# A hybrid mLSTM/GLA decoder block: the first MLP product as seven block products for eight

## What is computed

```python
hm = rmsnorm(x, mlp_norm_g[l]) @ w1[l]          # 1024 -> 4096
x = x + jnp.square(jax.nn.relu(hm)) @ w2[l]     # 4096 -> 1024
return rmsnorm(x, final_norm_g)
```

## Time and profile before

| what | value |
|---|---|
| runs | 2822.79, 2825.96, 2828.97 us; median 2825.96 |
| profiled execution | span 2824.3 us; the runs shown lie 1.5 us under to 4.7 us over it |
| PE / PEld busy | 2800.3 (99%) / 2330.9 us (83%) |
| DVE / ACT / POOL busy | 1812.8 (64%) / 1514.2 (54%) / 1057.3 us (37%) |
| DMA | 393.41 MB, mean 139 GB/s |

### The profile page before, as it was taken

One profiled execution on the slowest core, in us unless ns is written; L12 is line 12 of the kernel. 1 busy time (PEld: TensorE's weight loads), 2 busy tenths in 40 slices (PEclk: granted clock), 3 DMA queues, 4 the chain that ended last, 5 costly groups with the idle time before them and its releaser, 6 DMA issues.

```text
span 2824.3 us, 44962 instructions
## 1 busy us (share of the span) xinstructions
PE 2800.3 (99%) x15076; PEld 2330.9 (83%) x15076; DVE 1812.8 (64%) x3011; ACT 1514.2 (54%) x3126; POOL 1057.3 (37%) x1334
## 2 busy tenths in 40 slices
PE   8999999999999999999999999999999999999998
PEld 8888888788878888888888888888888888888887
DVE  6376774766686755457687674466668675545665
ACT  6554444556555444556565554465655644455553
POOL 5264574644345500234546320044435550023440
PEclk9999999999999999999999999999999999999999
DMA  6732586555552222355654222255556222234442
GB/s 217 249 105 68 175 292 235 186 173 147 150 196 83 73 93 90 100 177 153 175 164 145 74 83 90 90 157 169 144 150 201 83 73 93 90 102 144 150 149 82
DMA packets 185906, 393.41 MB, mean 139 GB/s; under 512 B 14224, under 2 KB 14368, under 8 KB 185664
## 3 DMA queue, kind: packets, MB, share of 16 engines
q1 hardware_dynamic: 160112, 309.89, 35.8%
q0 software_dynamic: 22880, 75.72, 8.0%
q10 hardware_dynamic: 2672, 4.76, 0.4%
HBM read 346.24 MB, written 33.59 MB: 134 GB/s over the span
## 4 chain that ended last, share of the span: by engine, by line
PE 97%; DVE 1%; issue 1%; DMA 1%; ACT 0%; DVEq 0%; POOL 0%; ACTq 0%
PE bank L1975 44%; PE work L1975 22%; PE bank L2342 17%; PE work L2342 3%; PE work L1989 1%; PE bank L2380 1%; PE work L2091 1%; PE bank L1989 1%; PE work L2129 1%; PE work L2037 1%; PE work L2151 1%; PE work L2240 1%; PE work L2244 1%; PE work L2239 1%; PE work L2223 1%
## 5 line engine op out<-in xcount | busy, mean ns | idle before, releaser
L899 ACT ACTIVATE w_hi<-raw 128x512 fp32r<-128x512 f32 x1156 | 724.7, 630 | 1018.9 <-PE bank L1975 515.8
L1413 DVE TENSOR_TENSOR w_lo<-raw,w_hi 128x512 fp32r<-128x512 f32 x657 | 475.8, 728 | 792.9 <-ACT w_hi L899 791.4
L1411 DVE SCALAR_TENSOR_TENSOR w_lo<-raw,w_hi 128x512 fp32r<-128x512 f32 x499 | 448.1, 918 | 95.3 <-ACT w_hi L899 94.1
L734 POOL TENSOR_TENSOR hr<-qk 128x256 f32<-128x256 f32 x60 | 44.3, 738 | 790.0 <-ACT qk L1287 790.0
L2342 PE MATMUL bank<-w_hi,h_hi 128*128 128x512 f32 x720 | 280.3, 389 | 0.1
L2342 PE MATMUL bank<-w_lo,h_hi 128*128 128x512 f32 x720 | 280.1, 389 | 0.0
L2342 PE MATMUL bank<-w_hi,h_lo 128*128 128x512 f32 x720 | 280.1, 389 | 0.0
L1975 PE MATMUL bank<-w_hi,x_hi 128*128 128x512 f32 x640 | 255.2, 399 | 0.0
L1975 PE MATMUL bank<-w_lo,x_hi 128*128 128x512 f32 x640 | 249.6, 390 | 0.0
L1975 PE MATMUL bank<-w_hi,x_lo 128*128 128x512 f32 x640 | 249.4, 390 | 0.0
L724 POOL TENSOR_TENSOR h_lo<-qk,h_hi 128x256 fp32r<-128x256 f32 x180 | 188.0, 1064 | 67.2 <-ACT h_hi L1300 67.2
(11 more groups left out here) (399 smaller groups left out, 6473.6 us busy)
## 6 DMA issues: line engine op xcount, KB each, us to landing
raw<-in_w_dram SPq DMA_DIRECT2D x226, 512.0 KB, 3.9
raw<-sums_dram SPq DMA_DIRECT2D x120, 512.0 KB, 3.8
raw<-in_w_in_dram SPq DMA_DIRECT2D x112, 512.0 KB, 3.6
raw<-in_w_out_dram SPq DMA_DIRECT2D x32, 512.0 KB, 4.1
raw<-kq_dram SPq DMA_DIRECT2D x32, 512.0 KB, 3.7
raw<-vo_dram SPq DMA_DIRECT2D x32, 512.0 KB, 3.7
xres<-in_x_dram POOLq DMA_DIRECT2D x16, 512.0 KB, 6.1
early_rows<-in_w_dram POOLq DMA_DIRECT2D x8, 1024.0 KB, 9.1
```

Source lines behind the costliest of these rows:

```text
L734: nc.gpsimd.tensor_tensor(diff[:, kt, :], quarter(0, 0, kt), quarter(0, 1, kt), ALU.subtract).then_inc(diff_ready, 1)
L899: nc.scalar.activation(w_hi[:, slot, :], raw[:, pair_slot, slot % 2, :], ACT.Copy).then_inc(slab_hi, 1)
L1411: ins = stt(out=w_lo[:, slot, :], in0=src, scalar=1.0, in1=hi, op0=ALU.mult, op1=ALU.subtract)
L1413: ins = tt(w_lo[:, slot, :], src, hi, ALU.subtract)
```

## The change

w1 gets what w2 had. A pass now has 28 slabs of w1 (seven products by four slabs) and 28 of w2; a w1 slab is used with 12 matmuls of 256 columns (`w1_product`), since x is cut into token halves of 256. x is turned into `xg` (f32), and in pass 0 POOL and ACT make its combinations and their parts once per group (`x_first_sums`, `x_later_sums`, `x_high`, `x_low`), DVE two of the low parts. Chained products share PSUM banks. Hidden is put together from them: ACT copies P1, P7 and P6 (`copy_product`), DVE adds P2, P5 and P4 (`add_hidden`), ReLU and square are DVE's in pass 0 (`squared_relu`) and ACT's in the other passes (`relu_pair`, `square_pair`); P3 is ACT's ReLU and DVE's square. In `hidden_sums` POOL also makes the low parts of P1. DVE's low parts of P7 move behind the start of the w2 product.

POOL now has 32 jobs of sums: four at the end of the prologue (before the mixer's distances), two between distances and products of the mixer (their buffer is xres, reloaded after them), sixteen through `early_rows`, six after `hidden_sums(0)`, four after `hidden_sums(1)`. `next_rows` and all 16 moves of `next_blocks` come before the `hidden_sums` in which they stood. The last pass of group 3 has w1 in seven products and w2 plain.

```diff
+W2_AT = PRODUCTS * HALF
+PASS_SLABS = 2 * W2_AT
...
-EARLY_SUMS, BEFORE_SUMS = 8, 14
+N_SUMS = 2 * HB * HALF
+ROWS_SUMS, FIRST_SUMS, BEFORE_SUMS, NEXT_SUMS = 4, 6, 22, 28
 Q_P1, Q_P7, Q_P6, Q_P2, Q_P5, Q_P4, Q_P3 = range(PRODUCTS)
...
-DVE_LOW = {Q_P1: 0, Q_P7: 1, Q_P2: 2}
-POOL_LOW = {Q_P6: 0, Q_P5: 1, Q_P4: 2, Q_P3: 3}
+WEIGHTS = (("plain", 0, 0), ("sums", 1, 1), ("sums", 0, 0), ("plain", 1, 0), ("sums", 0, 1), ("sums", 1, 0),
+           ("plain", 1, 1))
+DVE_LOW = {Q_P7: 0, Q_P2: 1}
...
+                if n < FIRST_SUMS:
+                    return xres[:, 2 * (n % 2):2 * (n % 2) + 2, :]
+                if n < BEFORE_SUMS:
+                    return early_rows[:, n % 4]
+                if n < NEXT_SUMS and n % 4 >= 2:
+                    return tok[:, 2 * (n % 2):2 * (n % 2) + 2, :]
...
+            def sums_by_two(first, last):
+                for n in range(first, last):
+                    weight_sums(n)
+                    if n + 1 < last and n > first:
+                        sums_done(pool, n - 1)
+                        load_quarters(n + 1)
+            pool.wait_ge(tok_ready, PRO_ROWS)
+            for n in range(2):
+                load_quarters(n)
+            sums_by_two(0, ROWS_SUMS)
...
+                def x_first_sums():
+                    for kt in range(HALF):
+                        pool.wait_ge(xg_ready, KT * g + kt + 1)
+                        nc.gpsimd.tensor_tensor(xdiff[:, kt, :], xg_quarter(0, 0, kt), xg_quarter(1, 0, kt),
+                                                ALU.subtract).then_inc(x_s3_ready, 1)
+                    for kt in range(HALF):
+                        x_low(Q_P1, kt, xg_quarter(0, 0, kt))
+                    for kt in range(HALF):
+                        pool.wait_ge(x_s3_ready, HALF * g + kt + 1)
+                        x_low(Q_P7, kt, xdiff[:, kt, :])
+                def x_later_sums():
+                    pool.wait_ge(x_op_lo_pool, N_X_POOL * g + HALF)
+                    for kt in range(HALF):
+                        pool.wait_ge(xg_ready, KT * g + HALF + kt + 1)
+                        pool.wait_ge(x_s3_ready, HALF * g + kt + 1)
+                        nc.gpsimd.tensor_tensor(xg_quarter(1, 0, kt), xg_quarter(1, 0, kt), xg_quarter(1, 1, kt),
+                                                ALU.add).then_inc(x_s1_ready, 1)
+                        pool.wait_ge(x_s1_ready, HALF * g + kt + 1)
+                        nc.gpsimd.tensor_tensor(xg_quarter(0, 0, kt), xg_quarter(1, 0, kt), xg_quarter(0, 0, kt),
+                                                ALU.subtract).then_inc(x_s2_ready, 1)
+                    pool.wait_ge(x_op_lo_pool, N_X_POOL * g + 2 * HALF)
+                    for kt in range(HALF):
+                        pool.wait_ge(x_s2_ready, HALF * g + kt + 1)
+                        nc.gpsimd.tensor_tensor(xdiff[:, kt, :], xg_quarter(0, 1, kt), xg_quarter(0, 0, kt),
+                                                ALU.subtract).then_inc(x_s4_ready, 1)
+                    for kt in range(HALF):
+                        x_low(Q_P5, kt, xg_quarter(1, 0, kt))
+                    for kt in range(HALF):
+                        x_low(Q_P4, kt, xg_quarter(1, 1, kt))
+                    for kt in range(HALF):
+                        pool.wait_ge(x_s4_ready, HALF * g + kt + 1)
+                        x_low(Q_P3, kt, xdiff[:, kt, :])
...
+                def hidden_sums(hb):
                     if hb >= 1:
                         pool.wait_ge(operand_hi, per_pass(g, N_HIGH, hb, 0))
                         pool.wait_ge(operand_lo_pool, per_pass(g, N_POOL_LOW, hb, 0))
                     for kt in range(HALF):
-                        pool.wait_ge(hidden_ready, per_pass(g, KT, hb, kt + 1))
+                        operand_low(Q_P1, hb, kt, quarter(0, 0, kt))
+                    for kt in range(HALF):
+                        block_ready(pool, g, hb, Q_P2, kt // 2)
+                        block_ready(pool, g, hb, Q_P4, kt // 2)
                         nc.gpsimd.tensor_tensor(diff[:, kt, :], quarter(0, 0, kt), quarter(0, 1, kt),
                                                 ALU.subtract).then_inc(diff_ready, 1)
-                    if between is not None:
-                        between()
-                    pool.wait_ge(operand_lo_dve, per_pass(g, N_DVE_LOW, hb, HALF))
+                    pool.wait_ge(operand_lo_pool, per_pass(g, N_POOL_LOW, hb, HALF))
...
+                if first:
+                    for n in range(ROWS_SUMS, FIRST_SUMS):
+                        sums_done(pool, n - 2)
+                        load_quarters(n)
+                    sums_by_two(ROWS_SUMS, FIRST_SUMS)
+                    for n in range(ROWS_SUMS, FIRST_SUMS):
+                        sums_done(pool, n)
+                    for i in range(NCH):
+                        pool.dma_start(xres[:, i, :], A["x"][i * P:(i + 1) * P, :]).then_inc(x_in, 16)
...
-                    for n in range(4):
+                    for n in range(FIRST_SUMS, FIRST_SUMS + 4):
                         load_quarters(n)
-                    for n in range(EARLY_SUMS):
+                    for n in range(FIRST_SUMS, BEFORE_SUMS):
+                        if n == FIRST_SUMS + 10:
+                            pool.wait_ge(pr_ready, 8 * g + 8)
                         weight_sums(n)
-                        if 2 <= n < 6:
+                        if FIRST_SUMS + 2 <= n < BEFORE_SUMS - 2:
                             sums_done(pool, n - 2)
                             load_quarters(n + 2)
-                    pool.wait_ge(norm_ss, PRO_ROWS + 16 * g + NCH)
...
-                    for n in range(8):
+                    for n in range(16):
                         move_blocks(n)
+                x_first_sums()
+                x_later_sums()
+                pool.wait_ge(norm_ss, PRO_ROWS + 16 * g + 8)
                 hidden_sums(0)
-                pool.wait_ge(norm_ss, PRO_ROWS + 16 * g + 8)
                 stand_alone(pool)
                 pool.dma_start(fin_g[:], A["final_norm_g"].partition_broadcast(P)).then_inc(fin_g_in, 16)
                 if first:
-                    for n in range(BEFORE_SUMS, N_SUMS):
+                    for n in range(BEFORE_SUMS, BEFORE_SUMS + 4):
+                        load_quarters(n)
+                    for n in range(BEFORE_SUMS, NEXT_SUMS):
                         weight_sums(n)
-                hidden_sums(1, next_rows)
+                        if n < NEXT_SUMS - 4:
+                            sums_done(pool, n)
+                            load_quarters(n + 4)
+                next_rows()
+                hidden_sums(1)
+                if first:
+                    for n in range(NEXT_SUMS, NEXT_SUMS + 2):
+                        load_quarters(n)
+                    sums_by_two(NEXT_SUMS, N_SUMS)
+                    for n in range(N_SUMS - 2, N_SUMS):
+                        sums_done(pool, n)
                 if final:
                     hidden_sums(2)
                     return
-                hidden_sums(2, next_blocks)
-                for n in range(8, 16):
-                    move_blocks(n)
+                pool.wait_ge(norm_ss, PRO_ROWS + 16 * g + 12)
+                next_blocks()
+                hidden_sums(2)
                 hidden_sums(3)
                 for i in range(NCH):
...
+                def x_high(q, kt=None):
+                    signal, n, src = {Q_P1: (xg_ready, KT * g + HALF, xg_half(0, 0)),
+                                      Q_P7: (x_s3_ready, HALF * g + HALF, xdiff),
+                                      Q_P6: (x_s2_ready, HALF * g + (kt or 0) + 1, xg_half(0, 0)),
+                                      Q_P2: (xg_ready, KT * g + KT, xg_half(0, 1)),
+                                      Q_P5: (x_s1_ready, HALF * g + HALF, xg_half(1, 0)),
+                                      Q_P4: (xg_ready, KT * g + KT, xg_half(1, 1)),
+                                      Q_P3: (x_s4_ready, HALF * g + HALF, xdiff)}[q]
+                    here = slice(0, HALF) if kt is None else slice(kt, kt + 1)
+                    act.wait_ge(signal, n)
+                    nc.scalar.activation(x_operand(q, 0)[:, here, :], src[:, here, :], ACT.Copy).then_inc(x_op_hi, 1)
...
+                    if r == KT + 4:
+                        x_high(Q_P1)
+                    if r == KT + 5:
+                        x_high(Q_P7)
+                for n in range(BEFORE_SUMS - 4, BEFORE_SUMS):
+                    sums_done(act, n)
...
+                def relu_pair(hb, q, tile):
+                    act.wait_ge(w1_added, added_no(g, hb, q, tile))
+                    nc.scalar.activation(hidden_pair(q, tile), hidden_pair(q, tile), ACT.Relu).then_inc(relu_done, 1)
+                def square_pair(hb, q, tile):
+                    act.wait_ge(relu_done, 6 * LAST * g + (6 * (hb - 1) + 2 * ADDED[q] + tile + 1))
```

(56 more changed lines are left out.)

581 lines of the change are left out of this document (345 added, 236 removed).

## The result

The kernel after takes **2978.0 us** by the median of 4 runs (2969.2 to 2980.8), the one before 2825.1 on the same chip: a ratio of 1.0535, interval 1.0517 to 1.0554. I had said 2890, between 2828 and 2935. The direction was right, the size was not. The profiled execution took 2980.3 us with a span of 2978.8, 154.5 more than the earlier trace rows. Executions of one kernel scatter more than before: up to 12 us here, for 6.

A forecast was written before the change was run, and what follows sets the result against it. PE's own work was taken as the bound, busy 2800 of 2824.3 us. Terms -51.2, -4.5, +8, +1.5, +32.5, +33, +18, +18, +6, +2.5 sum to +64: 2888, median 2890, range 2828 to 2935.

The forecast's parts named there:

- PE's work: w1 products, all 16 passes: 336 matmuls at 120.0 ns replace 192 at 226.7, 3.2 us less per pass, -51.2 us.
- rival E: PE's matmuls: a 256-wide one costs less than 120 ns, at best half of a 512-wide one; 2854 us, chance 0.05.
- The two long waits in group 0: Passes 1 and 2: PE waits 26 and 27 us for POOL's low part of P1; terms +32.5 and +33 us.
- The wait for x_first: Group 0, start of pass 0: sixteen jobs delay P1 to about 475 for 465 us; +8, between 3 and 12.
- The six jobs ahead of that I put at nothing: Group 0 before its MLP: PE's mixer matmuls cover these POOL jobs; nothing, or up to 5 us without that cover.
- DVE in the w2 product, 2 us: w2 products: added DVE work makes PE wait 2 us in each of 9 passes; +18 us, ends 0 and 36.
- the squeeze behind the two long waits: Group 0, passes 1 and 2: POOL's 16 us up to P6's low part exceed PE's 10.9; 5 us more each.
- DVE in pass 0: Pass 0, four groups: DVE's lag costs 0.6 us in w1 and 2 + 2 in w2; +18 us, ends 4 and 40.
- Moves: Pass 2, groups 1 and 2: one 9.3 us wait among sixteen moves makes POOL 3 us late; +6, ends 0 and 30.
- Pass 3's w1 product: Pass 3: turns and splits of the next x come closer together, but the ring covers them; no cost.
- Last pass: Plain w2 product begins with P4's block, needing addition, ReLU, square, high and low part in a row; +2.5 us.
- The stated signs: Wrong if PE's waits in group 0 passes 1 and 2 stay under 10 us, or groups 1 to 3 gain 13.

The follow-up runs named there:

- Run 2: Jobs 0 to 5 of group 0 left out of the kernel after, their slabs loaded as plain rows: 2964.6 us, ratio 1.0480.
- Run 10: POOL's sixteen sums of hidden tiles per pass made on 8 of 256 columns, from the kernel after: 2915.8 us, ratio 1.0314.
- Run 7: Kernel after with P3's squares and pass 0's ReLUs and squares on ACT, P6's high parts two steps later: 2971.9 us, ratio 1.0513.
- run 12: Kernel after with all 32 jobs left out and POOL's sums of hidden tiles on 8 of 256 columns: 2815.3 us, ratio 0.9961.
- runs 4, 9 and 10: From the kernel after, 4: P3's squares on ACT, 2970.7 us; 9: also P7's low parts on 8 of 256 columns, 2959.2 us; 10: see Run 10.

## Why the prediction was wrong, step by step

- **PE's work**, -51.2: right. 336 matmuls take 40.30 us, 120 ns each, so rival E is out. The formula of the Trainium skill that I set beside it ("TensorE: Matmul & The Clock Gate", section "Back-to-back issue gap") is given there for a matmul by itself; in this stream the trace has 120 ns where it gives 109.
- **The two long waits in group 0**: the mechanism is right, a queue of POOL behind which PE waits for the low part of P1. Its length was 14 us too short: from the start of the pass to its w2 product 73.1 and 74.8 us for 66.3 and 67.3, mostly as loads took longer to land than in the earlier trace rows. That the waits themselves measured 26.6 and 29.6 for 26 and 27 is luck, since PE came to them 6.2 and 4.9 us late. The wait for x_first measured 12.3 for 8, just over the end of my 3 to 12.
- **"The six jobs ahead of that I put at nothing"**: this step failed. I looked for cover in PE's matmuls, but who was short was DVE, whose instructions with two inputs in SBUF slow beside a job. Run 2 shows it: 20.8 us late at 401 us with these jobs and 2.8 without them in the two traces, and 12 to 27 late in the ten traces that have them. With the sixteen later jobs it is 21.8 at the start of the MLP, where I had allowed up to 5.
- **"DVE in the w2 product, 2 us"**: this step failed, and it is the larger one. The crowding stood in the text, with its hour (the first low part of P6 at 10.6 us, measured 10.9). But I priced it as a wait for one w_lo at the end of the ring and took P7's low parts only as 4 x 0.76 of load. They are operands with an hour of their own, 5.4 us into the product, and behind the squares the first was ready only 6.5 to 9.1 us into it: 25.8 us of PE's waits. The products of pass 1 lose 3.9 us (5.7 in group 0), the others 3.9 to 8.0, all together 80. Mine were 18, 16 (pass 0), 10 (the squeeze behind the two long waits) and 3 of slow clock, 47. The P7 low parts took 0.95 for 0.76, the two squares 1.22 for 0.75 to 1, and the w_lo between them 1.23, because all twelve sums fell on the same 12 us. A mean over the product (0.927) was the wrong price for its crowded start. I also left out the lower clock behind such waits, 10.3 us. Run 10 gives 62 of the 80 us to POOL's sums, 4.1 a product.
- **DVE in pass 0**: its w1 product loses 1.7 us a group for 0.6, and 2.7 more in group 0 behind the wait for x_first, for 1.5. Its w2 product, 5.7 to 6.3 for 4, is in the 80. Run 7 shows that the lag isn't tied to the squares on DVE.
- **Moves**, +6: pass 2's w1 product takes 43.5 and 41.3 us for 40.3 in groups 1 and 2, 4.2 in all. ACT's wait of 3.1 us for a slab is the way. This trace has the least: where that stage's code is the same, the other runs have 6.8 to 13.8.
- **Pass 3's w1 product**, put at nothing: 42.2 us in groups 0 to 2, 1.9 each. The cause stays open.
- **Last pass**, +2.5: measured 9.1. 4.7 are the wait for the low part that I had in mind, 1.4 the w1 product, and 2.9 the lower clock in its w2 product (0.91 in the mean for 0.96).
- The stated signs came true in part: waits in passes 1 and 2 far over 10 us, and groups 1 to 3 did not take their 13 us less. But I expected them to break even, and they lost 12 to 16.

What was missed in the trace, in the order of the list: 14 + 4 + 22 + 33 + 6 - 2 + 6 + 7 = 90 us, for the 91 between 2888 and the span of 2978.8.

The experiments meet it from the other side: 51 us of matmuls and 5 of the old wait and its clock gained; jobs 97, sums of hidden tiles 62, and what run 12 leaves over the ideal, 2815 - 2770 = 45 us. 2770 + 45 + 62 + 97 = 2974 for 2978. In run 12's trace I find 47 of this kind: 14 us in w2 products, 28 in the w1 products of passes 0, 2 and 3 (15 of these in pass 2, beside the moves) and 9 in the last pass, less 4 by which the MLP of group 0 starts sooner than before. No experiment takes these apart further.

What stays open: whether another order of the seven products, which makes P4's block sooner, would take the twelve sums from the start of the w2 product. It wasn't tried; by run 10 it could give about those 62 us, and the jobs alone cost more than the change saves. Open too is how the 97 us of the jobs divide between POOL's arithmetic, its waits for transfers and the traffic.

## What to carry to other kernels

An engine that is off the critical path isn't free work for its neighbour: price work given to POOL by what it does to DVE's instructions with two inputs in SBUF, and ask at each place whether DVE is the one that has no room, not whether PE is covered. Price a crowded stretch by the rows of its most crowded microseconds and by the hour at which each operand is wanted, not by means over the stage. A wait that measures what was forecast proves little if the engine came to it late; compare when it ended. When relief of the suspected engine gives back a third of it, look at who waits next before giving up the theory: runs 4, 9 and 10 together showed what none alone did.

## What the runs showed of the hardware

Unforeseen was what the form of copies inside SBUF can do to another queue. Sixteen copies of 8 partitions each, the same bytes as before in longer pieces, went with a load of another queue that took 27.9 us to land, against 12.8 at most; whether the few partitions or the long pieces do it is open. Also, the start of pass 0 in group 0 lay between 487.3 and 505.3 us in the profiled executions of kernels that are alike up to there, and most of that spread is there by 260 us, beside the first six jobs; the mixers of groups 1 to 3 agree within 2.2 us. The time spent beside jobs varies from run to run, and a single trace doesn't fix it. And nine waits of PE of 2.3 to 2.5 us in w2 products look alike, but the granted clock fell to 0.5 behind six of them, 1.7 us lost each time, and stayed at 1.0 behind three.
